# VectorE's state-space coefficients behind the first layer's norm, sine arguments and skip terms behind the first scan step

## The reference

```python
# first block, layer 2, its end
x_new = layer_norm(DEEPNORM_ALPHA * x + gate * y, ln_g, ln_b)

# second block, layer 1 (even_mixer), on hn = rms_norm(x, g)
z = hn @ w_in                              # q, k, v (512 wide each) and u (512)
q, k = partial_rope(q, positions), partial_rope(k, positions)   # cos/sin of positions
att = dilated_attention(q, k, v)
# s5_mixer: 32 groups of 16 channels, 64 complex states each
A  = complex(a_re, a_im);  dt = exp(log_dt)
a_bar = exp(A * dt)
b_bar = ((a_bar - 1) / A) * complex(b_re, b_im)
h_t = a_bar * h_(t-1) + b_bar @ u_t        # over 512 tokens
y = real(c_mat @ h) + d_skip * u
y = gelu(y); ssm = y * sigmoid(y @ w_glu)
mix = concat(att, ssm) @ w_out
```

## Time and profile before

| what | us |
|---|---|
| median of 3 runs (lowest, highest) | 2376.95 (2376.03, 2380.2) |
| the profiled execution, its own time | 2382.59 |
| its span, first to last instruction | 2380.8 |
| PE busy, DVE busy in the span | 2203.8, 1073.3 |
| ACT busy, POOL busy in the span | 668.7, 827.2 |
| granted TensorE clock, mean | 0.967 |

### The profile page before, as it was taken

The page is one execution under the profiler, slowest core; times in us unless marked ns, Lnnn a source line. Parts: engine busy times, 40 slices in busy tenths (PEclk is TensorE's granted clock), DMA queues, the critical chain, the costliest instruction groups (busy, mean ns, idle before and its releaser), DMA issues. The chain is left out here.

```text
span 2380.8 us, 28069 instructions
## 1 busy us (share of the span) xinstructions
PE 2203.8 (93%) x11735; PEld 1770.9 (74%) x11735; DVE 1073.3 (45%) x1645; ACT 668.7 (28%) x1030; POOL 827.2 (35%) x389
## 2 busy tenths in 40 slices
PE   5999898989999999997898889999998999999997
PEld 3887777856676868885755668888887578888886
DVE  2113664653666565668885533111126674111113
ACT  3223223324545454642102323100113343010101
POOL 1422013401323332227300225553544255545453
PEclk7999999999999999998999999999999999999999
DMA  9332114422111111112111112232322222223222
GB/s 298 74 111 71 54 54 114 118 89 89 36 36 36 36 36 36 54 45 89 40 54 36 54 53 72 90 105 89 107 89 89 73 86 89 89 93 102 90 96 80
DMA packets 174798, 187.47 MB, mean 79 GB/s; under 512 B 25601, under 2 KB 153937, under 8 KB 174545
## 3 DMA queue, kind: packets, MB, share of 16 engines
q1 hardware_dynamic: 164720, 175.42, 23.6%
q10 hardware_dynamic: 9376, 8.16, 1.2%
q0 software_dynamic: 576, 2.10, 0.2%
HBM read 183.56 MB, written 2.10 MB: 78 GB/s over the span
## 5 line engine op out<-in xcount | busy, mean ns | idle before, releaser
L2957 POOL TENSOR_TENSOR weights_lo<-weights_raw,weights_hi 128x2048 fp32r<-128x2048 f32 (+1 forms) x104 | 471.2, 4531 | 803.2 <-ACT weights_hi L1407 604.9
L689 PE MATMUL ring<-input_hi,weights_hi 128*128 128x512 f32 x784 | 305.6, 390 | 3.1 <-POOL weights_lo L2957 3.1
L691 PE MATMUL ring<-input_hi,weights_lo 128*128 128x512 f32 x784 | 305.0, 389 | 0.0
L690 PE MATMUL ring<-input_lo,weights_hi 128*128 128x512 f32 x784 | 305.0, 389 | 0.0
L2802 DVE CAST weights_hi<-weights_raw 128x2048 fp32r<-128x2048 f32 (+1 forms) x72 | 87.0, 1209 | 366.2 <-PE ring L691 173.9
L2948 POOL TENSOR_TENSOR h_w<-h_p 128x512 f32<-128x512 f32 x56 | 72.7, 1298 | 411.8 <-PE ring L998 304.4
L971 PE MATMUL obank<-acts,weights_raw 128*128 128x512 f32 x384 | 177.9, 617 | 0.6 <-issue 0.6
L689 PEld LDWEIGHTS ring<-input_hi,weights_hi 128*128 128x128 f32 x784 | 147.2, 188 | 34.2 <-issue 3.8
L690 PEld LDWEIGHTS ring<-input_lo,weights_hi 128*128 128x128 f32 x784 | 147.2, 188 | 30.8 <-issue 0.2
L691 PEld LDWEIGHTS ring<-input_hi,weights_lo 128*128 128x128 f32 x784 | 147.2, 188 | 30.5
L980 PE MATMUL obank<-weights_raw,acts 128*128 128x256 f32 x640 | 143.2, 381 | 0.0
(11 more groups left out here) (461 smaller groups left out, 4442.6 us busy)
## 6 DMA issues: line engine op xcount, KB each, us to landing
weights_raw<-in_w_ada SPq DMA_DIRECT2D x24, 1024.0 KB, 5.3
weights_raw<-in_ffn_w_gate SPq DMA_DIRECT2D x22, 1024.0 KB, 5.1
weights_raw<-in_ffn_w_up SPq DMA_DIRECT2D x22, 1024.0 KB, 5.2
weights_raw<-in_w_in_c SPq DMA_DIRECT2D x20, 1024.0 KB, 5.1
weights_raw<-in_ffn_w_down SPq DMA_DIRECT2D x16, 1024.0 KB, 5.0
weights_raw<-in_w_in_ab SPq DMA_DIRECT2D x9, 1024.0 KB, 7.5
weights_raw<-in_ev_w_in SPq DMA_DIRECT2D x8, 1024.0 KB, 5.5
weights_raw<-in_od_w_in SPq DMA_DIRECT2D x8, 1024.0 KB, 5.4
```

The lines of the kernel that those rows point to most:

```text
L689: pe.matmul(o, hi[:, k, ms], xh[:, k, t0:t0 + n], start=k == 0, stop=False)
L690: pe.matmul(o, hi[:, k, ms], xl[:, k, t0:t0 + n], start=False, stop=False)
L691: last = pe.matmul(o, lo[:, k, ms], xh[:, k, t0:t0 + n], start=False, stop=k == KD - 1)
L2957: pool.tensor_tensor(W_LO[slot][:, 0:kt, :], WR[:, slot, 0:kt, :], w_hi[:, 0:kt, :], ALU.subtract).then_inc(sem("w_lo"), 1)
```

## The change

Four places change. On DVE, `s5_weights` and `s5_inputs` come behind `tile_norms`, and the sine arguments and `s5_skips` come behind step 0: the arguments before `s5_readout`, the skips after it. On ACT, the two sines come behind the copy of the first `eqk` quarter. The scratch tile into which ACT squares (`C_JUNK`) moves from `w + 17408`, where the raw `b` lies (`SBRAW`), to `w`, as `b` is now still needed during the norm.

```diff
-            C_JUNK, E_JUNK, F_JUNK = (view(at, n, D, name="junk") for at, n in ((w + 17408, 1), (w + 15360, 1), (x_at + 4 * D, TL)))
+            C_JUNK, E_JUNK, F_JUNK = (view(at, n, D, name="junk") for at, n in ((w, 1), (w + 15360, 1), (x_at + 4 * D, TL)))
...
-            act.wait_ge(sem("rope_arg"), 1)
-            link(act.activation(COSP, COSP, ACT.Sin))
-            act.activation(SINP, SINP, ACT.Sin).then_inc(sem("rope_tab"), 1)
             for c in range(4):
                 pair(f"eqk{c}.lat", EQK, c, 0)
+                if c == 0:
+                    act.wait_ge(sem("rope_arg"), 1)
+                    link(act.activation(COSP, COSP, ACT.Sin))
+                    act.activation(SINP, SINP, ACT.Sin).then_inc(sem("rope_tab"), 1)
...
             link(last)
+            dve.wait_ge(sem("bc_in"), 64)
+            tile_norms(y1_norm, 1, C_DIAG, HT, V_NPRE)
             s5_weights()
             s5_inputs()
-            dve.wait_ge(sem("bc_in"), 64)
-            tile_norms(y1_norm, 1, C_DIAG, HT, V_NPRE)
...
             s5_turned_c()
             s5_powers()
-            dve.wait_ge(sem("pos_in"), 16)
-            link(dve.tensor_copy(A1, EPOS.bitcast(I32)))
-            link(dve.tensor_scalar(A1, A1, colt(0), None, ALU.mult))
-            sine_args(A1, SINP, COSP, A2, "rope_arg")
-            dve.wait_ge(sem("rope_arg"), 1)
-            s5_skips()
...
                 s5_step(st)
                 if st == 0:
+                    dve.wait_ge(sem("s5_h"), 1)
+                    dve.wait_ge(sem("pos_in"), 16)
+                    link(dve.tensor_copy(A1, EPOS.bitcast(I32)))
+                    link(dve.tensor_scalar(A1, A1, colt(0), None, ALU.mult))
+                    sine_args(A1, SINP, COSP, A2, "rope_arg")
+                    dve.wait_ge(sem("rope_arg"), 1)
                     s5_readout()
+                    s5_skips()
                     dve.wait_ge(sem("rope_tab"), 1)
```

## The result

| | before | after |
|---|---|---|
| median of 16 runs each (lowest, highest), us | 2378.06 (2373.15, 2382.28) | 2383.85 (2380.61, 2391.26) |
| the profiled execution: time, span | 2382.59, 2380.8 | 2381.93, 2380.1 |

The ratio is 1.0029, 95% interval 1.0019 to 1.0039: 6.9 us slower by the ratio, 5.8 by the medians. The prediction was 2385.5 in a range of 2380 to 2389, slower by 8.5.

A forecast was written before the change was run, and what follows sets the result against it. DVE was taken to set the pace up to 1224.35 us, PE after it. The powers' later end (6.7) plus DVE's waiting for turns (1.8) gave +8.5 us on the median 2376.95: 2385.5, range 2380 to 2389.

The forecast's parts named there:

- the powers' later end: DVE's `s5_powers` ends at 1165.3 instead of 1158.6, adding 6.7 us.
- rival (a): Mild contention: small DVE operations slip between POOL's, powers end by 1162; +3.8 to +5.2 us, about 2381.5; chance 0.16.
- The norm's move: On DVE, the second column half's norm starts 6.3 us earlier, at 1099.7; L1175 then starts at 1130.4.
- The coefficients' turns: After the norm, each small `s5_weights` operation on DVE waits a whole POOL operation: 15 x 1.15 = 17.3 us.
- shared speed: DVE keeps 0.44 of its free speed beside POOL; powers end at 1161.2, +4.4 us.
- The new path: From powers' end to second scan step: turns, input product, step 0, arguments, readout, skips; 1.8 us from waiting for turns.
- B + 49.6: Start of DVE's second scan step, B being the powers' end: 1214.9 against 1206.42, +8.5 us.
- PE's early start: PE gets its first input product at 1174.2, 4.3 us early, given back before L1136, which waits for the readout.
- rival (c): PE and not DVE carries the chain and keeps its lead of 4.3 to 9.0 us: 2368 to 2373; chance 0.12.
- (b): The shift is absorbed downstream by a wait not tied to PE: about 2377.5; chance 0.10 together with no effect.

The follow-up runs named there:

- e8_coefs_args_late_gate: Kernel before with coefficients behind the norm, sine arguments behind step 1's kernel products, POOL's last twelve doublings held until the powers are done; ratio 0.9962, median 2366.18 us.
- e1: Kernel before with only the coefficients moved behind the norm and ACT's scratch tile moved; ratio 1.0031.
- e4: Kernel before with POOL's last eighteen table doublings left out and filled with constants; ratio 0.9998.
- e5: Kernel before with only the sine arguments moved behind step 1's kernel products and ACT's sines behind the second `eqk` copy; ratio 0.9989.
- e9_before_gate: Kernel before with only POOL's last twelve doublings held back until DVE's powers are done; ratio 1.0019.
- the light kernels: The changed kernel and the kernel before, each with POOL's last eighteen table doublings replaced by constants; ratios 1.0014 and 0.9998 against before.
- e3_after_light_pool: Changed kernel with POOL's last eighteen table doublings left out and filled with constants; ratio 1.0014 against the kernel before.

## Why the prediction was right, and what was mis-sized

The path was right; one term of the sum, the powers' later end, was forecast at 6.7 us and measured 4.0. The stage's 5.7 us lie between the +5.2 at which rival (a), mild contention, ended and the +6 at which the forecast began; the medians give 5.8 and the ratio 6.9. The time alone doesn't choose between the two; the rows of the coefficients show something of each.

- **The norm's move: right.** First join predicted at 1099.7, seen at 1099.8; last `normed` 1129.4 against 1128.9; L1175 at 1130.4 against 1129.9 (1126.09 + 3.77).
- **The coefficients' turns: right that they cost turns, wrong that each costs one.** I had 15 operations of `s5_weights` pay a turn each (17.3 us) and `s5_inputs` almost none (4.8). It was 10.3 and 10.0. Some `s_par` operations slip in between two of POOL's (0.18 us at 1126.83 above), which is what rival (a) said, so nine of POOL's passed during `s5_weights` and the others were still there for `s5_inputs`, which ended 0.6 us after the last of them (1145.32 against 1144.72). Here the stretch was as long as POOL's operations lasted, and not as many turns as DVE had operations. 10.3 is just above the 10 at which I would have called myself wrong on it.
- **The powers' end: the term of the sum that was mis-sized.** Predicted 1165.3, 6.7 later than before; it was 1162.6, 4.0 later, between my 1161.2 for a shared speed and the forecast. Of the 2.7, 1.8 is the coefficients (20.3 for 22.1), 0.5 the norm's end, the rest the powers (12.2 for 12.5, 1146.62 to 1158.85). Measured by this term alone, the rival of mild contention (powers by 1162) was nearer than the forecast.
- **The new path: right.** B + 49.6 predicted, 1208.39 - 1158.85 = 49.5 seen, with the first step's start at B + 10.9 (11.0). Two terms in it were off by 1.6 us each in opposite directions, and that they cancel is luck: the 32 turns took 5.4 us where I had 3.8, the 16 behind them 1.9 where I had 3.5.
- **PE: right.** Its wait before L1127, none inside the turns, 3.37 before L1136 and a wait before the second half are as predicted; the stop before L1127 is 2.7 instead of 4.9, as the powers came sooner. The third `eqk` starts at 1230.1, not 1233. That PE's early start would be given back decided the sign against rival (c).
- **The end: right.** 4.0 + 1.7 = 5.7 us in the stage against 6.7 + 1.8 = 8.5; the time moved by 5.8 (medians) or 6.9 (ratio). Nothing absorbed it, so (b) falls. In the two profiled executions part of the shift seems to go behind the third `eqk`: that product takes 15.67 us before and 14.69 after, at granted clocks of 0.89 and 0.95 by the windows that follow; in e8_coefs_args_late_gate, with the same 1.9 us wait ahead of it as before, it took 13.97 at 1.00, as it did behind the same wait in e1, e4 and e5; in e9_before_gate it took 15.67 again. So the product runs at either speed behind the same wait, and nothing shows that the change gave something back there.

One stretch each (length, busy and count of PE, PEld, DVE, ACT, POOL, then the granted clock), of before:

```profile
1224.35:1240.02 15.67, 15.67 (x34) 6.91 (x35) 9.95 (x17) 0.00 (x0) 0.00 (x0) 0.89 0.00 1
```

in the PE timeline of e9_before_gate that product is

```profile
1230.18 15.67 PE L572 MATMUL ring<-acts,weights_raw 128*128 128x512 f32 x32 [1.89 <-DVE acts L2671]
```

of the same product in e8_coefs_args_late_gate:

```profile
1208.69:1222.66 13.97, 13.97 (x34) 6.32 (x35) 12.07 (x19) 1.26 (x2) 0.00 (x0) 1.00 0.00 1
```

and of after, the same product and the turns:

```profile
1226.32:1241.01 14.69, 14.69 (x34) 6.68 (x35) 9.95 (x17) 0.00 (x0) 0.00 (x0) 0.95 0.00 0
...
1158.90:1164.28 5.38, 5.38 (x34) 5.38 (x35) 2.06 (x2) 1.02 (x1) 0.00 (x0) 0.68 0.37 128
```

- **What I did not say.** I told contention as something that the change brings. It was there before, on the powers, and by the stages of the light kernels cost about the same (4.9 against 4.7 us). The loss that remains like with like, 5.9 us, is the order. My sum was right in total since it compared with the real trace of before, in which the powers' turns are contained, and took the powers at 12.5 us after.

## What to carry to other kernels

Before work is moved out from between two stages, ask what it hides under: here 12.8 us of DVE work lay under 30 us of PE products or ended just behind them, and moved behind them it was path. Where two engines take turns, the cost follows the operations that the other one has left, so moving one's own work mostly chooses which part pays; hold the rival's work back until it stands beside something that isn't late (and move away what it would stand beside next). Two moves around the same gap don't add up, and one that loses alone can belong to a gain (the coefficients' move in the last kernel): time each alone and together.

## What the runs showed of the hardware

- A plain tensor_scalar of 128x512 on DVE, SBUF to SBUF, takes 0.43 us alone and 1.15 beside POOL operations of 1.2 (e9_before_gate); an operation with two SBUF inputs takes 1.4 to 1.75 there and in the powers of before, 0.69 alone. POOL's own operation grows from 1.05 to 1.2 to 1.6. So it isn't only DVE operations with two inputs that pay.
- A reciprocal of 128x16 in the middle of the stretch took 0.25 us beside POOL's 128x512 operations, as in e3_after_light_pool, where POOL had none of them.
- The 32 turns took 5.38 us right behind PE's stop of 2.68 us, at a granted clock of 0.68 (row above), and 3.66 to 3.93 in the kernels in which PE came to them straight from L1175. So the clock was low for part of the stretch right behind the stop; the forecast had such a loss only in its range, as 1.5 us. In the windows of after it is back at 1.00 from 1164.28 on.
